# Latent attention with cached keys turned in 32x32 blocks by VectorE and scored on sixteen array tiles

## The reference, cut to what matters

```python
def _mla_sample(x, lat_pages, rope_pages, page_table, w_in, q_norm, kv_norm, w_uq, w_ukv, w_out):
    ...
    lat_past = lat_pages[page_table].reshape(B, past, MLA_KV_RANK)
    rope_past = rope_pages[page_table].reshape(B, past, MLA_ROPE)
    ...
    q_lat = jnp.einsum('bqhn,rhn->bqhr', q_nope, w_uk)
    sc = (jnp.einsum('bqhr,bkr->bhqk', q_lat, lat_all)
          + jnp.einsum('bqhd,bkd->bhqk', q_rope, rope_all)).astype(jnp.float32) * MLA_SCALE
    ...
    p = jax.nn.softmax(jnp.where(mask, sc, -jnp.inf), axis=-1)
    o_lat = jnp.einsum('bhqk,bkr->bqhr', p.astype(lat_all.dtype), lat_all)
    o = jnp.einsum('bqhr,rhv->bqhv', o_lat, w_uv).reshape(B, T, MLA_HEADS * MLA_V)
```

## Time and profile before

| | us |
|---|---|
| median of 3 runs | 2698.49 |
| lowest, highest | 2693.58, 2698.68 |
| profiled execution | 2698.88 |
| its span | 2697.2 |
| TensorE busy in the span | 2634.7 |
| VectorE, ScalarE busy | 1529.4, 1161.6 |
| GpSimd busy | 302.1 |

### The profile page before, as it was taken

How to read it: one execution, slowest core, us unless ns; L and a number is a source line. 1 busy time by engine, 2 the same in 40 slices (tenths; PEclk the granted TensorE clock), 3 DMA queues, 4 the chain that set the end, 5 groups by cost and what they waited for, 6 DMA issues and landing times.

```text
span 2697.2 us, 51800 instructions
## 1 busy us (share of the span) xinstructions
PE 2634.7 (98%) x22023; PEld 2496.1 (93%) x22023; DVE 1529.4 (57%) x1891; ACT 1161.6 (43%) x1577; POOL 302.1 (11%) x305
## 2 busy tenths in 40 slices
PE   7999999999999999999999999999999999999998
PEld 6999987999999986699999999799999999989998
DVE  4556855655565545465555554465556558656654
ACT  4334644533444444353443443253344446444442
POOL 1000005100200045010010001010020000052000
PEclk9999999999999999899999999999999999999999
DMA  5445523454544645444455463354455455234543
GB/s 191 160 145 166 157 84 104 156 164 142 178 157 147 196 130 166 127 156 159 148 168 164 148 200 114 117 181 163 145 168 172 139 172 164 84 97 156 171 137 99
DMA packets 415625, 404.24 MB, mean 150 GB/s; under 512 B 14786, under 2 KB 411950, under 8 KB 415086
## 3 DMA queue, kind: packets, MB, share of 16 engines
q1 hardware_dynamic: 411348, 397.43, 46.6%
q0 software_dynamic: 4096, 4.20, 0.5%
HBM read 385.20 MB, written 16.39 MB: 149 GB/s over the span
## 4 chain that ended last, share of the span: by engine, by line
PE 92%; DVE 4%; ACT 2%; issue 1%; DMA 0%; SPq 0%; DVEq 0%; ACTq 0%
PE psum L379 22%; PE psum L380 22%; PE psum L381 22%; PE psum L541 2%; PE psum L545 2%; PE psum L542 2%; DVE w_lo L361 1%; PE psum L2792 1%; PE psum L1153 1%; PE psum L1170 1%; PE psum L2154 1%; PE psum L2805 1%; PE psum L1165 1%; ACT w_hi L344 1%; PE psum L1248 1%
## 5 line engine op out<-in xcount | busy, mean ns | idle before, releaser
L361 DVE TENSOR_TENSOR w_lo<-raw,w_hi 128x2048 fp32r<-128x2048 f32 (+2 forms) x362 | 745.0, 2058 | 515.6 <-ACT w_hi L344 515.4
L379 PE MATMUL psum<-xn_hi,w_hi 128*128 128x288 f32 x3232 | 963.0, 298 | 8.3 <-DVE w_lo L361 7.3
L380 PE MATMUL psum<-xn_lo,w_hi 128*128 128x288 f32 x3232 | 955.0, 295 | 0.0
L381 PE MATMUL psum<-xn_hi,w_lo 128*128 128x288 f32 x3232 | 951.7, 294 | 0.0
L344 ACT ACTIVATE w_hi<-raw 128x2048 fp32r<-128x2048 f32 (+2 forms) x350 | 598.7, 1710 | 800.9 <-PE psum L381 737.4
L379 PEld LDWEIGHTS psum<-xn_hi,w_hi 128*128 128x128 f32 x3232 | 607.1, 188 | 15.8 <-issue 5.9
L381 PEld LDWEIGHTS psum<-xn_hi,w_lo 128*128 128x128 f32 x3232 | 610.2, 189 | 0.0
L380 PEld LDWEIGHTS psum<-xn_lo,w_hi 128*128 128x128 f32 x3232 | 608.4, 188 | 0.6
L380 PE MATMUL psum<-h_lo,w_hi 128*128 128x288 f32 x1408 | 415.5, 295 | 0.0
L379 PE MATMUL psum<-h_hi,w_hi 128*128 128x288 f32 x1408 | 415.0, 295 | 0.0
L381 PE MATMUL psum<-h_hi,w_lo 128*128 128x288 f32 x1408 | 414.9, 295 | 0.0
(11 more groups left out here) (583 smaller groups left out, 3155.7 us busy)
## 6 DMA issues: line engine op xcount, KB each, us to landing
raw<-w_ffn_up SPq DMA_DIRECT2D x176, 1024.0 KB, 5.1
raw<-w_ffn_down SPq DMA_DIRECT2D x64, 768.0 KB, 4.4
raw<-w_ffn_down SPq DMA_DIRECT2D x64, 640.0 KB, 4.0
raw<-gdn_w_in SPq DMA_DIRECT2D x32, 1024.0 KB, 5.7
raw<-mlstm_w_in SPq DMA_DIRECT2D x12, 1024.0 KB, 5.4
raw<-gdn_w_out SPq DMA_DIRECT2D x8, 1024.0 KB, 5.6
raw<-cache_mla_latent SPq DMA_DIRECT2D x64, 128.0 KB, 2.5
a_split<-cache_mla_latent SPq DMA_DIRECT2D x64, 128.0 KB, 2.2
```

The source lines that it names most:

```text
L361: dve.tensor_tensor(spread(w_lo[slot(u, i)], u), packed(raw[u % NRAW], u), spread(w_hi[slot(u, i)], u).bitcast(F32), ALU.subtract).then_in ...
L379: pe.matmul(out, wh[:, k, c], hi(k), start=st, stop=False)
L380: pe.matmul(out, wh[:, k, c], lo(k), start=False, stop=False)
L381: last = pe.matmul(out, wl[:, k, c], hi(k), start=False, stop=sp_)
```

## The change

Cached keys are no longer transposed on TensorE. VectorE transposes blocks of 32x32 in place of that: five instructions a sequence, each over 128 partitions x 1024 numbers, from the page buffers to latD and ropD. In a block the 32 tokens of a partition quarter change places with 32 of the 256 (or 64) key numbers. So partition quarter q of latD holds the keys of tokens 32 q to 32 q + 31 of each page, in 8 pieces of 32 numbers (and 2 of ropD), and a score is a sum of ten products of 32 rows. sample_scores makes them: for each piece c, each quarter q and each group j of four pages one product of 32 rows, 32 query columns and 128 keys, from row tile q to column tile j, in bank q. That is 160 products on sixteen tiles. The queries must then lie on all four quarters: the query product is made four times, once to each quarter, with the operands exchanged, and VectorE turns it in 32x32 blocks to QLD; rotary queries are laid on the quarters by products with parts of the identity (QRD). Own-token scores keep a 128-row form (QL, QRO), built by ScalarE.

Further: latD and ropD are single, and pages_turned(b + 1) on VectorE waits for the scores of b; RSLOTS becomes 2; prompt probabilities and head outputs move from bank 3 to bank 4; the division by the sum (two scalings) and the copy to PVs move from VectorE to ScalarE; the exponential of the mixing weights comes behind the last head on ScalarE; the order of the loop on TensorE and VectorE is new.

```diff
-            ropes = [carve(f"a_rop{s}", [P, NP, ROPE]) for s in range(2)]
+            latD, ropD = carve("a_latd", [P, NP, KVR // 32, 32]), carve("a_ropd", [P, NP, ROPE // 32, 32])
+            ropes = [carve("a_rop0", [P, NP, ROPE])]
...
-        LSLOTS, RSLOTS = 4, 3
+        LSLOTS, RSLOTS = 4, 2
...
                 elif b >= RSLOTS:
-                    once(pool, "a_lat_turned", 10 * (b - 2))
+                    once(pool, "a_latd", 5 * (b - RSLOTS) + 5)
...
+            for h in range(MH):
+                once(pe, "a_k", h // 2 + 1)
+                for q in range(4):
+                    last = pe.matmul(psum[quarter(q), 4 + h // 2, h % 2 * KVR:(h % 2 + 1) * KVR], smp(qnT[:, h, :]),
+                                     WkT[:, h, :], start=True, stop=True)
...
             for b in range(NB):
                 if b + 1 < NB:
-                    pages_turned(pe, b + 1)
-                head_turned(pe, b)
+                    head_scores(pe, b + 1)
                 probs_turned(pe, b)
...
+                head_turned(pe, b)
+                sample_attend(pe, b)
                 head_attend(pe, b)
                 if b + 1 < NB:
-                    head_scores(pe, b + 1)
-                sample_attend(pe, b)
+                    sample_scores(pe, b + 1)
...
         def sample_scores(pe, b):
 
-            once(pe, "a_ev_a", 5 * b + 5)
-            once(pe, "a_ev_d", 5 * b + 5)
+            once(pe, "a_latd", 5 * b + 5)
             if b > 0:
                 once(pe, "a_sp", b)
...
+            for c in range(10):
+                for q in range(4):
+                    for j in range(4):
+                        if c < 8:
+                            old, new = latD[quarter(q), 4 * j:4 * j + 4, c, :], QLD[quarter(q), c, b].rearrange("p h t -> p (h t)")
+                        else:
+                            old, new = ropD[quarter(q), 4 * j:4 * j + 4, c - 8, :], QRD[quarter(q), c - 8, b, :]
+                        last = pe.matmul(psum[quarter(j), q, 0:P], new, old, start=c == 0, stop=c == 9)
             last.then_inc(sem("a_ssc_done"), 1)
...
+        def pages_turned(dve, b):
+
+            if b == 0:
+                once(dve, "a_ql_done", 4)
+            else:
+                once(dve, "a_ssc_done", b)
+            once(dve, f"a_lat_in{b % LSLOTS}", 16 * NP * (b // LSLOTS + 1))
+            for q in range(4):
+                dve.transpose(latD[:, 4 * q:4 * q + 4].rearrange("p j c t -> p (j c t)"),
+                              page_bufs[b % LSLOTS][q // 2][:, q % 2 * 1024:q % 2 * 1024 + 1024]).then_inc(sem("a_latd"), 1)
+            dve.wait_ge(sem(f"rope_in{b % RSLOTS}"), 16 * NP * (b // RSLOTS + 1))
+            dve.transpose(ropD[:].rearrange("p j c t -> p (j c t)"), ropes[b % RSLOTS].rearrange("p j r -> p (j r)") if b % RSLOTS
+                          else ropes[0][:].rearrange("p j r -> p (j r)")).then_inc(sem("a_latd"), 1)
...
             for b in range(NB):
-                if b + 1 < NB:
-                    lat_out(dve, dve.tensor_copy, 10 * (b + 1) + 1).then_inc(sem("a_ev_d"), 1)
-                scaled(b)
-                if b + 1 < NB:
-                    for f in range(3, 10, 2):
-                        lat_out(dve, dve.tensor_copy, 10 * (b + 1) + f).then_inc(sem("a_ev_d"), 1)
+                sample_max(b)
+                inverse(b)
...
                 if b + 1 < NB:
-                    sample_max(b + 1)
+                    pages_turned(dve, b + 1)
                     low(b)
                     masked(b + 1)
-                    attended(b)
```

More of the change, by code:

```diff
@@ L2691, in pe_mla @@
                 last.then_inc(sem("a_v_done"), 1)
[L2692 to L2698, removed]
+            for h in range(MH):
[3 more added lines that the diff above has]
+                                     WkT[:, h, :], start=True, stop=True)
+                if h % 2 == 1:
+                    last.then_inc(sem("a_ql_done"), 1)
+            once(pe, "a_v", 3)
             for t, (cols, _, _) in enumerate(token_tiles):
@@ L2708, in pe_mla @@
             last.then_inc(sem("a_tok_turned"), 1)
+            once(pe, "a_v", 4)
             once(pe, "a_q", 4)
-            once(pe, "a_ql", 1)
+            for c in range(2):
+                for q in range(4):
+                    last = pe.matmul(psum[quarter(q), 3, c * MH * NS:(c + 1) * MH * NS], ident[0:ROPE, 32 * c:32 * c + 32],
+                                     smp(qrT[:]).rearrange("p h (b t) -> p b h t", b=NB), start=True, stop=True)
+            last.then_inc(sem("a_qr_done"), 1)
+            once(pe, "a_qld", 4)
             head_scores(pe, 0)
-            once(pe, "a_v", 4)
+            once(pe, "a_qlc", 1)
+            own_scores(pe)
             once(pe, "a_tok", 1)
-            pages_turned(pe, 0)
-            own_scores(pe)
-            once(pe, "a_qr2", 1)
+            once(pe, "a_qrd", 1)
             sample_scores(pe, 0)
@@ L2756, in head_turned @@
             for j in range(3):
-                last = pe.transpose(psum[:, 3, j * P:(j + 1) * P], pm[:, j * P:(j + 1) * P], ident)
+                last = pe.transpose(psum[:, 4, j * P:(j + 1) * P], pm[:, j * P:(j + 1) * P], ident)
             last.then_inc(sem("a_p_turned"), 1)
@@ L2772, in own_scores @@
                 for rc in range(2):
[L2773 to L2774 removed]
+                    pe.matmul(own, QL[:, rc, b, :], smp(ckvT[:, rc, :]), start=rc == 0, stop=False)
+                last = pe.matmul(own, QRO[:, b, :], smp(krT[:]), start=False, stop=True)
             last.then_inc(sem("a_own_done"), 1)
[L2777 to L2793 removed]
@@ L2847, in samples_folded @@
                 half = slice(e * KVR, (e + 1) * KVR)
-                pe.matmul(psum[:, 4, half], own_pT[:, e * P:(e + 1) * P], ctok[0:NS, 2, :], start=True, stop=False)
+                pe.matmul(psum[:, 3, half], own_pT[:, e * P:(e + 1) * P], ctok[0:NS, 2, :], start=True, stop=False)
                 if e == 1:
@@ L2851, in samples_folded @@
                 for b in range(4):
-                    last = pe.matmul(psum[quarter(b), 4, half], fold[:, 4 * e + b, :], PVs[:, 4 * e + b, :],
+                    last = pe.matmul(psum[quarter(b), 3, half], fold[:, 4 * e + b, :], PVs[:, 4 * e + b, :],
                                      start=False, stop=True)
@@ L3036, in dve_mla @@
                                 ).then_inc(sem("a_k"), 1)
+            for q in range(4):
+                once(dve, "a_ql_done", q + 1)
+                for h in (2 * q, 2 * q + 1):
+                    last = dve.transpose(QLD[:, :, :, h, :], psum[:, 4 + q, h % 2 * KVR:(h % 2 + 1) * KVR])
+                last.then_inc(sem("a_qld"), 1)
             once(dve, "a_tok_turned", 1)
```

138 lines of the change are left out of this document (45 added, 93 removed).

## The result

The changed kernel takes **2721.95 us** (median of 4 runs, 2716.71 to 2724.43) against 2698.59 for the kernel before in the same comparison: a ratio of 1.0086, with a 95% interval of 1.0064 to 1.0107. It is slower by 23 us. The prediction said 2693.5, with a range to 2721; it has the wrong sign and the range misses by 1 us. The profiled execution took 2721.41 us with a span of 2719.7.

A forecast was written before the change was run, and what follows sets the result against it. TensorE was taken to bound the loop before, GpSimd's issuing of rotary rows after. From 2698.9 us, 5.3 came off by the last scores' start and 0 in the tail: 2693.5 us, range 2687 to 2721.

The forecast's parts named there:

- The score burst: TensorE's cached scores of one sequence: 160 products, 320 records, taking 2.3 us at full clock and 4.3 at half.
- the two bounds: Score burst on TensorE: 2.3 us if all sixteen tiles run side by side, 9.2 if row quarters don't overlap.
- a slower instruction stream in a burst of 640 instructions: Score bursts on TensorE: an uncertainty of 2 us within the likeliest case's own range of 2688 to 2698.
- The transposes: VectorE gains five transposes of 128x1024 a sequence, 1.2 us each, 6.0 us together; 8.5 us busy a sequence.
- The loop of waits: Single latD chains scores, maximum, reciprocal, transposes, next scores: period from 13.31 to about 10.1 us, 22 us saved alone.
- GpSimd: Issuing rotary rows at 7.49 us a half with two buffers: scores(7) start at 1100.0, so the gain is 5.3 us.
- The tail: From last scores to first output product: 23.4 to 28.0 us, taken as 27 against 26.97 before, so a gain of 0.
- The late exponential: In the tail, the exponential of the mixing weights stands behind the last head on ScalarE; no size of its own.
- row quarters don't overlap, or the burst starves: Rival, chance 0.10: scores on TensorE take 9.2 us, the period 16.7, the kernel 2721; decides from 5.8 us a burst.
- dear transposes: Rival, chance 0.12: VectorE's five transposes at 2.3 us each make the period 15.6 us and the kernel 2713.
- GpSimd slowed: Rival, chance 0.04: VectorE's transposes stop GpSimd for 6 of each 15 us; twelve halves take 36 us more, kernel 2730.
- GpSimd isn't the bound: Rival, chance 0.07: 7.49 us is pacing by waits, VectorE's loop sets the end; a gain of 26 us, kernel 2673.

The follow-up runs named there:

- the triple burst: The changed kernel with the score burst of the fourth sequence alone done three times over (960 records, 1920 instructions in place of 640): 2736.88 us, one run.
- the variant with the early exponential: The changed kernel with bursts cut in two, two early transposes, the head's product ahead of the second part and the mixing weights' exponential ahead of the last head: 2704.52 us.
- the cut in two: The changed kernel with products 0 to 3 behind the previous sequence's turned probabilities and 4 to 9 behind its values: 2746.85 us.

## Why the prediction was wrong, point by point

1. *The score burst: the step that failed.* I took 2.3 us at full clock, 4.3 at half. It is 5.8 to 9.3 us between the first and the last record, 7.1 on average. Of the two bounds, 2.3 and 9.2 us, I chose by the array, because the nearest rows were about tiles side by side; these have 16 to 128 records each, so at most 256 instructions. In the words of the prediction, "a slower instruction stream in a burst of 640 instructions" was worth 2 us in all, with no row behind it. The stops, which are the supply of instructions, are worth 1.6 to 4.9 us in each burst but the first. The pace adds 1.8 us a burst at full clock (12.8 ns a record in place of 7.3: 4.1 us); how much of that is instructions too, the runs don't show.
2. *The transposes*: 1.20 us forecast, 1.20 to 1.21 measured. VectorE busy for 8.5 us a sequence forecast, 8.2 measured.
3. *The loop of waits*: VectorE's part was nearly right (7.5 us forecast from the end of a burst to the next, 6.96 measured in the one period that it set, 1071.40 to 1084.06). TensorE's was wrong, and this is the second step that failed. I wrote that its rest, some 6 us, lies beside the transposes. At half clock it is 9.5 us and longer than they are, so that burst and rest together set the period in all periods but that one. The clock fell where TensorE's stops and waits are: before, it worked almost without a pause and had full clock; in the triple burst the clock falls after the first stop. Stops alone don't do it: in the variant with the early exponential the clock stays full from 1028 to 1103 with stops of 0.8 to 1.5 us. No run takes clock and stops apart, and how much of the 23 us is clock and how much stop stays open.
4. *GpSimd*: the pace of 7.49 us was right (7.47 measured, twice), the end of the loop with short bursts too (1099.4 against 1100.0, in part by luck), and the wait for the rotary rows appears in two of the three fastest variants of the changed kernel, those with half the products and with the early exponential. In the changed kernel it isn't the bound, since 16.35 us a sequence is longer than 15.0.
5. *The tail*: 27 forecast, 31.0 measured; the last burst alone takes 8.0 us in place of 2.3 to 4.3. The late exponential, which I named and priced at nothing of its own, is about 2 us by the trace.

Together: the profiled execution takes 27.9 us longer than forecast (2721.4 against 2693.5), 19.8 of it until the last scores start (1119.8 against 1100.0), 4.0 in the tail and 4.0 in later sub-layers, which I had at nothing.

**The rivals.** The second one, "row quarters don't overlap, or the burst starves", comes nearest: by it the scores of the last sequence start at 1125 (measured 1119.8), the period is 16.7 us (16.35) and the kernel takes 2721 (2721.95). Its named threshold of 5.8 us a burst is just where the measured ones begin. Of its two causes the second is shown. The first, row quarters one after the other, is wrong, as 12.8 ns a record is far from 29; that they overlap in part only isn't excluded. That its total fits so well is luck: it adds 9.2 us of burst to VectorE's 7.5, and what happened is 7.1 us of burst and TensorE's own rest of about 9. I gave it 0.10, and argued against it from the array rows alone; nothing in my views spoke of instructions. What was to be had: the page's row on the instruction queue, and the count of 640 instructions for 2.3 us, which no stretch of the trace before comes near; there the fastest 640 instructions of TensorE in a row take 9.6 us. The other rivals (dear transposes, GpSimd slowed) are refuted by points 2 and 4, and "GpSimd isn't the bound" by the run with half the products.

The Trainium skill, "Runtime: NRT & Kernel Launch", section Instruction fetch mechanics, says that instructions are refilled in blocks of 256 while the current one is executed, and that the cost of crossing a block's end is mostly hidden because dispatch is slower than the refill. This case's traces agree with the block (stops exactly 128 records apart) and with the fetching ahead (in most bursts of the changed kernel the packet starts 0.9 to 1.6 us after the block before it began to be used). They don't agree with the rest: 3.75 us for a block against 1.6 us of use.

## What to carry to other kernels

Count instructions as well as cycles: 12 products became 160, and here bursts of 640 instructions, each under 7 ns, ran dry, and those of 320 did not. There is no safe length in between by these runs: how soon a burst runs dry depends on where the blocks end, mostly after 430 to 540 instructions, but after 300 in the last burst. Put such a burst between long products, but follow first what queues behind each moved piece on the other engines: the cut in two cost 25 us in one order, and with two transposes and the head's product ahead it gave 16. Look also at what is transferred meanwhile: behind weights of 1 MB the block came some 3 us later. And when a step is made faster, look for the engine next in line; here it was GpSimd at 7.47 us a half sequence, which kept even a burst of half the products at no gain.

## What the runs showed of the hardware that I had not expected

- A block of 256 instructions takes 3.5 to 4.3 us to arrive when TensorE asks for nothing but instructions. Its packet takes 0.9 to 1.6 us, and TensorE goes on 1.2 to 1.6 us after it has landed, in all 97 stops. The stop's place is fixed in the program: it moves by nine records per sequence from the second on, in all runs alike.
- The stops of 4.3 to 5.7 us occur once or twice in eight of the runs, and in each of them the DMA engines are full (share 0.95 or more) until the packet of instructions starts, while the weights of the output projection are in transfer. No run moved these transfers, so the link is read from the traces and not tested.
- On sixteen 32x32 tiles, 128 columns take 12.8 ns a record and 64 columns 9.8: small products don't become cheaper in proportion.
- A 32x32 block transpose of 128x1024 float32 takes 1.20 us on VectorE, 1.17 ns a column. GpSimd keeps its 4.62 us for eight transfers beside it in nine of twelve halves; the other three are broken by pauses of 0.3 or 2.8 us, at the same places as in the kernel before.
